# Even mixer of a hybrid trunk: values inside a projection chunk, transposes ahead of scores, attention and taps ahead of the eviction

## What is computed

```python
def short_conv(a_x, a_b, a_c, conv_w):
    z = a_c * a_x
    zp = jnp.pad(z, ((0, 0), (CONV_W - 1, 0), (0, 0)))
    y = sum(conv_w[j] * zp[:, j:j + L] for j in range(CONV_W))
    return a_b * y
...
s = jnp.einsum('bcqhgd,bckhd->bchgqk', qr, kall) + bias      # scores: 16 meta keys and two chunks of 64
p = sink_softmax(s, sink[None, None, :, :, None, None])
out_r = jnp.einsum('bchgqk,bckhd->bcqhgd', p, vall)          # values
...
def even_mixer(u, w_in, conv_w, sinks, w_out, rel_bias):
    a_x, a_b, a_c, q, k, v = split_cols(u @ w_in, ...)
    y_a = short_conv(a_x, a_b, a_c, conv_w)
    y_b = window_attention(q, k, v, sinks, rel_bias)
    return jnp.concatenate([y_a, y_b], axis=-1) @ w_out
```

## Time and profile before

| | us |
|---|---|
| median of 3 runs | 1975.96 |
| lowest, highest | 1975.44, 1976.32 |
| span of the profiled execution | 1973.9 |
| PE busy in it | 1929.5 (98%) |
| DVE busy | 900.4 (46%) |
| ACT busy | 598.9 (30%) |
| POOL busy | 60.7 (3%) |

### The profile page before, as it was taken

How to read it: one execution, slowest core, us unless ns; L and a number is a source line. 1 busy time by engine, 2 the same in 40 slices (tenths; PEclk the granted TensorE clock), 3 DMA queues, 4 the chain that set the end, 5 groups by cost and what they waited for, 6 DMA issues and landing times.

```text
span 1973.9 us, 33852 instructions
## 1 busy us (share of the span) xinstructions
PE 1929.5 (98%) x13966; PEld 1826.8 (93%) x13966; DVE 900.4 (46%) x1141; ACT 598.9 (30%) x810; POOL 60.7 (3%) x70
## 2 busy tenths in 40 slices
PE   6999999999899999999999999999999999999997
PEld 6999999998799999999999999999998888888885
DVE  5444443346745444443344444333656654444333
ACT  5322222224424222222232222222423432323221
POOL 0000000001000000000000000000034000000001
PEclk8999999999999999999999999999999999999998
DMA  4323223242122222323323233233321232232321
GB/s 169 107 85 95 85 81 96 90 124 66 55 71 90 89 92 85 94 79 89 93 94 92 88 87 91 84 92 93 94 67 63 86 96 95 90 93 90 97 88 43
DMA packets 53121, 175.70 MB, mean 89 GB/s; under 512 B 6524, under 2 KB 8860, under 8 KB 52928
## 3 DMA queue, kind: packets, MB, share of 16 engines
q1 hardware_dynamic: 52816, 174.71, 29.0%
q10 hardware_dynamic: 240, 0.07, 0.0%
HBM read 171.35 MB, written 3.41 MB: 89 GB/s over the span
## 4 chain that ended last, share of the span: by engine, by line
PE 94%; DVE 3%; ACT 1%; DMA 0%; issue 0%; SPq 0%; DVEq 0%; ACTq 0%
PE psum L1079 91%; DVE wl L708 1%; ACT wh L386 1%; DMA raw<-in_w_gate_up 0%; PE psum L1101 0%; PE psum L1336 0%; ACT probs L519 0%; DVE ss L718 0%; DVE x L1068 0%; PE psum L1220 0%; ACT sq L401 0%; SPq L312 0%; PE psum L1346 0%; PE psum L1348 0%; PE psum L1347 0%
## 5 line engine op out<-in xcount | busy, mean ns | idle before, releaser
L1079 PE MATMUL psum<-xh,wh 128*128 128x264 f32 (+1 forms) x3024 | 701.3, 302 | 8.2 <-DVE xl L725 8.2
L1079 PE MATMUL psum<-xl,wh 128*128 128x264 f32 (+1 forms) x3024 | 699.1, 301 | 0.0
L1079 PE MATMUL psum<-xh,wl 128*128 128x264 f32 (+1 forms) x3024 | 697.2, 301 | 0.0
L386 ACT ACTIVATE wh<-raw 128x1024 fp32r<-128x1024 f32 x255 | 270.1, 1060 | 876.1 <-PE psum L1079 873.3
L708 DVE TENSOR_TENSOR wl<-raw,wh 128x1024 fp32r<-128x1024 f32 x327 | 405.1, 1239 | 259.5 <-ACT wh L446 155.6
L1079 PEld LDWEIGHTS psum<-xh,wh 128*128 128x128 f32 x3024 | 486.6, 189 | 28.5 <-DVE wl L708 8.2
L1079 PEld LDWEIGHTS psum<-xl,wh 128*128 128x128 f32 x3024 | 485.1, 189 | 18.3 <-issue 0.5
L1079 PEld LDWEIGHTS psum<-xh,wl 128*128 128x128 f32 x3024 | 484.3, 189 | 17.7
L1079 PE MATMUL psum<-hh,wh 128*128 128x264 f32 (+1 forms) x1424 | 335.5, 303 | 1.5 <-DVE hl L894 1.5
L1079 PE MATMUL psum<-hh,wl 128*128 128x264 f32 (+1 forms) x1424 | 335.1, 303 | 0.0
L1079 PE MATMUL psum<-hl,wh 128*128 128x264 f32 (+1 forms) x1424 | 334.9, 303 | 0.0
(11 more groups left out here) (209 smaller groups left out, 651.3 us busy)
## 6 DMA issues: line engine op xcount, KB each, us to landing
raw<-in_w_gate_up SPq DMA_DIRECT2D x176, 512.0 KB, 3.6
raw<-in_w_down SPq DMA_DIRECT2D x64, 448.0 KB, 3.3
raw<-in_w_down SPq DMA_DIRECT2D x32, 512.0 KB, 3.5
raw<-in_od_in SPq DMA_DIRECT2D x21, 512.0 KB, 3.6
raw<-in_ev_in SPq DMA_DIRECT2D x18, 512.0 KB, 3.7
raw<-in_ev_out SPq DMA_DIRECT2D x8, 512.0 KB, 3.6
raw<-in_od_out SPq DMA_DIRECT2D x8, 512.0 KB, 3.6
x<-in_x_t SPq DMA_DIRECT2D x8, 264.0 KB, 5.4
```

Source lines behind the costliest of these rows:

```text
L386: act.activation(wh[:, slot, :], raw[:, slot, :], ACT.Copy).then_inc(wh_ready, 1)
L1079: last = pe.matmul(dst, weights[:, slot, w], moving[:, k, tok], start=start and p == 0, stop=stop and p == 2)
```

## The change

Nothing is computed otherwise, and no instruction is added or dropped. Four orders change:

- PE: `values(s-8)` moves from behind chunk s to the middle of it, ahead of k = 4 (through `between`, which `from_x` now calls for each k; the table of the first block uses the same hook as before). Behind the chunk come first `transpose_probs(s-7)`, then `scores(s-5)`.
- ACT: `attention_high(s-8)` and the exponentials move ahead of the slot's split of the weights, the exponentials one slot later (group s-6 where it was s-5). The copies of the transposes stay behind the split.
- DVE: `attention_low(s-8)` moves ahead of the wait for the chunk and its eviction. `softmax_scores(s-5)` moves from behind the split of the weights to ahead of it.
- DVE: `conv` is cut in two: `conv_taps` ahead of the wait for the chunk, `conv_gate` (the product by b) right behind the eviction.

```diff
@@ ACT @@
             for s in range(EV_TILES):
+                if 8 <= s < 17:
+                    attention_high(s - 8)
+                if 6 <= s < 15:
+                    exponents(s - 6)
                 next_high(CHUNK["ev_in"] + s)
...
                 if 7 <= s < 16:
+                    turned(s - 7)
@@ DVE @@
-            def conv(j):
+            def conv_taps(j):
                 dve.wait_ge(z_ready, j + 1)
-                dve.wait_ge(acc_free, TILE["ev_in"] + 8 + 3 * j + 1)
...
+            def conv_gate(j):
+                dve.wait_ge(acc_free, TILE["ev_in"] + 8 + 3 * j + 1)
+                dve.tensor_tensor(conv_b[:, :], conv_x[:, :], conv_b[:, :], ALU.mult).then_inc(conv_ready, 1)
...
+                if 8 <= s < 17:
+                    attention_low(s - 8)
+                if gated:
+                    conv_taps((s - 8) // 3)
                 dve.wait_ge(chunk_done, CHUNK["ev_in"] + s + 1)
                 scaled(two(dst_ev[s]), acc_slot(t)).then_inc(acc_free, 1)
+                if gated:
+                    conv_gate((s - 8) // 3)
+                if 5 <= s < 14:
+                    softmax_scores(s - 5)
                 next_low(CHUNK["ev_in"] + s)
...
-                if 8 <= s < 17:
-                    attention_low(s - 8)
                 if 6 <= s < 15:
                     softmax_probs(s - 6)
-                if 5 <= s < 14:
-                    softmax_scores(s - 5)
-                if s >= 8 and (s - 8) % 3 == 0:
-                    conv((s - 8) // 3)
@@ PE @@
                 for k in range(KT):
-                    if between and k in (1, 4):
-                        table_products(k == 4)
+                    if between:
+                        between(k)
                     last = passes(outs, n % RING, k, xh, xl, k, k == 0, k == KT - 1)
...
-                from_x(CHUNK["ev_in"] + s, t, 1, first=s == 0)
+                from_x(CHUNK["ev_in"] + s, t, 1, first=s == 0, between=lambda k: values(s - 8) if k == KT // 2 and 8 <= s < 17 else None)
...
-                if 8 <= s < 17:
-                    values(s - 8)
+                if 7 <= s < 16:
+                    transpose_probs(s - 7)
                 if 5 <= s < 14:
                     scores(s - 5)
-                if 7 <= s < 16:
-                    transpose_probs(s - 7)
```

More of the change, by code:

```diff
@@ L500, in _ @@
                     act.activation(v_far[0:N_META, 3, :], psum[0:N_META, 7, 3 * P:4 * P], ACT.Copy).then_inc(vt_ready, 1)
-                if 8 <= s < 17:
[L502 to L510, removed]
-                if 5 <= s < 14:
[L512 to L521, removed]
-                if 7 <= s < 16:
[L523 to L528, removed]
-                        far = N_META if b == 0 else 80
-                        act.activation(pt_far[0:far, :], psum[0:far, 7, :], ACT.Copy).then_inc(pt_ready, 1)
-                        act.activation(pt_near[:, :], psum[:, 6, :], ACT.Copy).then_inc(pt_ready, 1)
+                if 7 <= s < 16:
+                    turned(s - 7)
                 if s >= 8 and (s - 8) % 3 == 0:
@@ L899, in _ @@
             for s in range(EV_TILES):
+                gated = s >= 8 and (s - 8) % 3 == 0
+                t = TILE["ev_in"] + s
                 if s >= 9 and (s - 9) % 3 == 0:
                     conv_low((s - 9) // 3)
-                t = TILE["ev_in"] + s
+                if 8 <= s < 17:
+                    attention_low(s - 8)
+                if gated:
+                    conv_taps((s - 8) // 3)
                 dve.wait_ge(chunk_done, CHUNK["ev_in"] + s + 1)
                 scaled(two(dst_ev[s]), acc_slot(t)).then_inc(acc_free, 1)
+                if gated:
+                    conv_gate((s - 8) // 3)
+                if 5 <= s < 14:
+                    softmax_scores(s - 5)
                 next_low(CHUNK["ev_in"] + s)
@@ L1081, in passes, with from_x @@
                 return last
-            def from_x(n, tile, v=None, more=0, real=False, first=False, between=False):
+            def from_x(n, tile, v=None, more=0, real=False, first=False, between=None):
                 pe.wait_ge(wl_ready, more + (n + 1))
@@ L1118, in ffn @@
                         pe.wait_ge(var_ready, v + 1)
-                    from_x(base + c, t + c, v, real=real, first=c == 0, between=q == 0 and c == 1)
+                    from_x(base + c, t + c, v, real=real, first=c == 0, between=tables if q == 0 and c == 1 else None)
                     if c == 1:
@@ L1162, in table_products, with tables @@
                 last.then_inc(table_done, 1)
+            def tables(k):
+                if k in (1, 4):
+                    table_products(k == 4)
             ffn(0, 0)
```

30 lines of the change are left out of this document (27 added, 3 removed).

## The result

The changed kernel takes **1963.32 us** (median of four runs, 1962.91 to 1963.42) beside 1976.14 for the kernel before in the same session (1975.44 to 1979.64). The ratio is 0.9932, with an interval of 0.9918 to 0.9947. The span of the profiled execution went from 1973.9 to 1961.4. The forecast was 1962.2, so it was 1.1 us too low, and the time lies inside the range.

What follows compares the result with a forecast made beforehand. PE bounds the kernel, held up by its feeders' order: 10.2 + 1.5 + 1.5 + 0.7 + 1.3 - 1.4 = 13.8 us saved, span 1973.9 to 1960.1, plus 2.06 gives 1962.2 us; range 1959.0 to 1967.5.

Steps and rivals of the forecast that it cites:

- What bounds it: Whole span: PE is 94% of the last-ending chain; its mixer waits come from an order, not a lack of speed.
- The waits ahead of the transposes (10.2): Even mixer: PE's eight waits for DVE's `attention_low` result `hl` go, gaining 10.2 us.
- their overlap (0.7): Listed durations run 0.07 past the next start, so the ten waits cost 0.7 us more than their idle time.
- The slot step: Mixer, PE from slot to slot: about 8.9 us, where it was 9.8 to 10.6.
- The break (0.15 a slot): Splitting nine chunks for values costs 0.15 us each, 1.4 in all; bounds 0 and 4.0.
- the first rival: Break at 0.44 a slot and clock dip still there: gain 9.9 us, time 1966.1; chance 0.12.
- The first values (1.5): Slot 8: PE's wait ahead of the first `values` for ACT's copy to `pt_far` goes, gaining 1.5 us.
- the clock (1.3): Behind slot 8: the fall to 0.50 of full clock goes with the waits, gaining 1.3 us; other bound 0.
- DVE's walk: DVE's work through mixer slots: `attention_low` ends 1.5 us ahead of the chunk's end, 0.4 in slots 9, 12, 15.
- The end (1.5, with 1.7 in hand): Out-projection, k = 7: the wait for the convolution's last `hl` goes, gaining 1.5 us with 1.7 in hand.
- DVE late: DVE later than walked in the mixer slots: 1965.2 to 1970.2; chance 0.08 with some gain, 0.02 with all eaten.
- The clock falling in every slot: Nine broken chunks: small products halve the clock, costing 41 us, time 2003.6; chance 0.03.

Runs made afterwards that it cites:

- run 3: Changed kernel with PE's order of before, so only ACT's and DVE's parts of the change: 1963.81 us, ratio 0.9933 against the kernel before.
- run 5: Changed kernel with scores ahead of the transposes again on PE, values still in mid-chunk: 1962.12 us, one run.
- run 6: Kernel before with ACT's copies of the transposes ahead of the exponentials of the same slot: 1976.37 us, ratio 0.9996.
- run 1: Kernel before with `attention_low` ahead of the split of the weights on DVE: 1975.45 us, ratio 0.9994.
- run 7: Changed kernel with two unused extra DVE passes over 128 x 528 ahead of `attention_low` in slots 9 to 15: 1965.37 us.
- run 4: Changed kernel with the convolution whole again, taps and gate at the end of gated slots on DVE: 1972.94 us, ratio 0.9975 against the kernel before.
- run 2: Kernel before with PE's part alone, values in mid-chunk and transposes ahead of scores: 2029.79 us, ratio 1.0267.
- run 9: Kernel before with two swaps, `attention_low` ahead of DVE's weight split and ACT's copies ahead of the exponentials: 1969.86 us, ratio 0.9963.
- run 8: Changed kernel, PE's order of before, ACT's high part behind its split, `attention_low` behind eviction and gate: 1964.92 us, ratio 0.9938 against the kernel before.
- run 11: Changed kernel with scores ahead of the transposes, the kernel of run 5 timed again: 1962.03 us, ratio 0.9921 against the kernel before.

## Why the prediction was right, and where it was off

**What bounds it: right.** The waits were an order and not a lack of speed. Run 3 shows it most plainly: the same instructions, only ACT's and DVE's in another order, give 0.9933. The prediction counted on the half chunk behind the values as cover for the hand-over; run 3 leaves PE's order as it was and has 9.99 of the 11.83 us, so the cover of half a chunk removed only the last waits, 2.8 us, and with its own price won 1.84.

**The waits ahead of the transposes (10.2) and their overlap (0.7): right in kind, 0.5 too large with the break.** Slots 9 to 15 were to gain 9.61 + 0.49 - 1.05 + 0.26 = 9.31 and gained 8.83, by the table. (The 0.26 are the slow pair of matmuls, which stands at the start of slot 9.) The slot step was put at 8.9 and is 9.06. The two terms behind this were off in opposite directions. The idle time overstated what can be had: slot 11 had 0.92 idle and 0.07 of overlap, but its unbroken length without a wait is 8.98 (run 3), so of its 9.78 only 0.80 were to be had. That is 0.19 too much in each of the five slots with scores, 0.95 in all, against a break that was 0.07 too dear in seven slots, 0.49. Part of a wait hides time that PE needs anyway (the transposes start 1.11 behind the scores when nothing is waited for, where the listed duration of the scores is 0.97).

**The break (0.15 a slot): too dear in most slots.** It is 0.00 by run 5, 0.08 with the order of transposes and scores that this kernel has. The bound of 0 was the right one there, and the reason was in the prediction, only too small: the change from values to scores was put "somewhere under 0.1" and is 0.20. In slot 16, with neither scores nor transposes behind the chunk, no price shows (13.04 and 13.01). In slot 8, where the values are 16 x 16 products and the scores take 0.91 behind them already, it was too cheap: 0.20 in run 5 and 0.30 here (8.53 and 8.63 against 8.33 unbroken). The bad end of the first rival, 0.44, is excluded.

**The first values (1.5) and the clock (1.3): right.** Slot 8 was to gain 3.12 (1.5 + 0.59 + 0.14 + 1.04 - 0.15; the other 0.26 of the clock's 1.3 lie in slot 9) and gained 2.97. Run 3 tells the terms apart, since its chunk 8 is unbroken and has no wait and a clock of 1.00 around it. From there to chunk 9, on PE:

```profile
464.56 0.51 PE L1089 MATMUL psum<-xh,wh 128*128 128x264 f32 x2
...
472.89 0.49 PE L1089 MATMUL psum<-xh,wh 128*128 128x264 f32 x2
```

It takes 8.33 where before took 11.60, 3.27 less, which is what the four terms of gain add up to. The missing 0.15 is the break. The wait goes by ACT's new order together with DVE's; run 6 shows that moving ACT's copy alone doesn't do it. One reading was wrong: the clock was low before the second wait, not behind it. The scores between the two waits already took 1.25, and in run 1, with the first wait alone, the transposes of slot 8 took 1.53 all the same.

**DVE's walk: its rule held, its numbers were too gloomy.** `attention_low` was to end 1.5 us ahead of the chunk in plain slots and 0.4 in 9, 12 and 15. In the trace it is 1.5, 0.95 and 2.07 in those three, and 1.55 to 2.0 in the others. Slot 12 on DVE:

```profile
508.77 0.41 DVE L883 TENSOR_TENSOR hl<-psum,hh 128x256 fp32r<-128x256 f32 x1
510.32 0.71 DVE L745 TENSOR_TENSOR conv_c<-psum,rms 128x528 f32<-128x528 f32 x1 [1.14 <-PE psum L1089]
```

The low part is done at 509.18, the chunk at 510.13. It is the case the walk described, and the walk was 0.55 short: the slot is 0.16 longer than the 8.9 assumed, and DVE's pieces overlap by some tenths. Slots 9 and 15 aren't that case. Slot 9 is longer, since its values take 1.47 instead of 1.03, and slot 14, ahead of 15, has no scores for DVE. The walk took one pattern for three places whose work differs. Run 7 confirmed the corrected walk in where PE waits and for how long, though it cost 3.1 us in all for 2.1 of listed waits.

**The end (1.5, with 1.7 in hand): right.** The last `hl` of the convolution, DVE in slot 17 and behind it:

```profile
550.24 0.71 DVE L745 TENSOR_TENSOR conv_b<-psum,rms 128x528 f32<-128x528 f32 x1 [0.73 <-PE psum L1089]
...
552.74 0.70 DVE L901 TENSOR_TENSOR hl<-conv_b,hh 128x528 fp32r<-128x528 f32 x1
```

It is ready at 553.4, 3.4 us behind the chunk; k = 7 comes 5.1 behind it. All behind the mixer gained 1.85 where 1.57 were forecast. Counted in steps, the wait accounts for 1.79 of it: the out-projection's second chunk started 7.64 behind its first (560.62 to 568.26) and starts 5.85 behind it now (549.97 to 555.82).

**What the prediction left out: the start.** It took the rest of the span as fixed. Another 1.18 us came in there, which is nearly the whole error of the forecast. Mixer and end gained 13.7 where 13.8 were forecast.

**The rivals.** DVE late: not here, and run 4 is what it looks like (1972.94). The clock falling in every slot: excluded for this kernel, with 1.00 from 450 to 561 us. The psum-queue section of the Trainium skill's "TensorE: Matmul & The Clock Gate", cited in the prediction, says that brief pauses between groups make the clock swing; in this kernel there were no pauses to swing on, and products of small shapes in mid-chunk didn't lower it. In some of the kernels that kept waits (before, runs 1, 2, 4, 6 and 9) the clock did fall, in others (runs 3, 7 and 8) it stayed at 1.00: the last section has the numbers.

## What to carry to other kernels

An idle time of the bounding engine can hang on several engines' orders at once: before pricing one swap, walk each feeding engine through the slot and ask what is late next, since here the swaps of runs 1 and 6 were worth 1.15 and -0.31 us apart and 6.38 together. In an engine's list, put work whose input is long ready ahead of the wait for the next input (the taps: 8.5 us), and a small hand-over that another engine needs ahead of a large pass that nobody needs yet. Moving the consumer earlier pays only once its feeders are early: that part alone cost 2.7%, and behind the others it took 1.84 us off the stretch.

## What the runs showed of the hardware that was not expected

- **The clock behind a wait.** In the mixer it fell behind waits of 1.5 (slot 8, before and run 1), 2.31 (run 6), 2.02 and 2.61 (run 4), 1.28 (run 9, slot 8) and even 1.10 (run 1, slot 10), but not behind single waits of 1.86, 1.85 and 1.74 in later slots of before, nor behind the 1.80 of run 7, nor anywhere in the kernels without waits there. Some of the waits behind which it fell follow small products and some a whole chunk, so no rule is shown. It may also go with scatter: the kernel before ran from 1975.4 to 1980.0 in all sessions, run 6's from 1974.8 to 1978.9, run 4's from 1970.8 to 1973.7, while the changed kernel and runs 3, 8 and 11 each stayed within 1.1 us in a session. That the clock is the cause is not shown; run 2, with the lowest clock of all, has two executions 0.3 us apart.
- **Small products of one shape take PE longer next to some shapes than to others.** Scores take 1.11 behind the values, but 0.91 behind the chunk (run 5, where the transposes follow as they do there) or behind the transposes (the changed kernel); behind the 16 x 16 values of slot 8 they take 0.91 too (run 3). Transposes take 0.79 to 0.83 up to a chunk and 0.96 up to the scores; values 1.03 up to either.
- **A stationary operand of 16 rows isn't cheaper than one of 80.** The values of the first block of queries took 1.47 us (487.50 to 488.97) for the same count of instructions; PE's timeline, slot 10 of the changed kernel:

```profile
487.50 0.43 PE L1258 MATMUL psum<-pt_far,v_far 16*64 16x128 f32 x4
...
488.97 0.51 PE L1089 MATMUL psum<-xh,wh 128*128 128x264 f32 x2
```

  It is the same in both kernels; why was not tried.
- **The first 40 us vary by 1.6 us between executions** (37.37 to 38.96 up to the first sums of squares), with a granted clock from 30 to 40 us of 0.54 in one profile, 0.65 and 0.66 in others. For a gain of some tenths, as in run 11, the time between two inner points of the trace decides where the total can't.
